# Two mixture-of-experts layers on one core: experts' outputs weighted per slot and added to their tokens' rows in memory, in place of stores, gathers and sums

## The reference, cut to what matters

```python
def hier_moe(h, ...):                       # t: 512 x 1024
    # group by softmax over 4, then the best 2 of the group's 4 experts
    comb = sum(one_hot(expert_id, 16) * weights[..., None])     # 512 x 16, two non-zero a row
    def step(acc, xs):
        wg, wu, wd, cw = xs
        y = (silu(t @ wg) * (t @ wu)) @ wd
        return acc + y * cw[:, None], None
...
h_lat = h_lat + g2 * hier_moe(modulate(h_lat, norm2_g[i], sh2, sc2), ...)   # i = 0, 1
```

## Time and profile before

| | us |
|---|---|
| median of 3 runs | 2244.4 (2242.2 to 2245.37) |
| the profiled execution, its own time | 2244.1 |
| its span, first to last instruction | 2242.5 |
| PE matmuls busy | 2044.5 (91%) |
| DVE busy | 794.9 (35%) |
| ACT busy | 580.6 (26%) |
| POOL busy | 715.6 (32%) |
| mean granted TensorE clock | 0.951 of full |
| transfers: q1 (SP) | 38502 packets, 217.48 MB |
| q0, the only software queue (POOL's) | 27920 packets, 103.82 MB |
| q10 (ACT) | 4608 packets, 16.78 MB |
| data moved | 339.29 MB, 151 GB/s over the span |

### The profile page before, as it was taken

The page is one execution under the profiler, slowest core; times in us unless marked ns, Lnnn a source line. Parts: engine busy times, 40 slices in busy tenths (PEclk is TensorE's granted clock), DMA queues, the critical chain, the costliest instruction groups (busy, mean ns, idle before and its releaser), DMA issues. The chain is left out here.

```text
span 2242.5 us, 23210 instructions
## 1 busy us (share of the span) xinstructions
PE 2044.5 (91%) x7824; PEld 1099.2 (49%) x7824; DVE 794.9 (35%) x1596; ACT 580.6 (26%) x1205; POOL 715.6 (32%) x1055
## 2 busy tenths in 40 slices
PE   7999999999999999999997697995999699778995
PEld 5555555555564555555542355653444344344442
DVE  1434534432123444433315358533222300442223
ACT  3234331234113442221511114521111211111110
POOL 4766766756766676600000031000110100001101
PEclk9999999999999999999998798996999799878997
DMA  7234343234343244360112600016995621055994
GB/s 301 84 113 150 133 145 119 95 127 145 127 150 111 90 166 144 119 266 38 48 75 104 220 16 22 1 46 279 349 366 210 226 75 38 0 226 227 369 366 165
DMA packets 71119, 339.29 MB, mean 151 GB/s; under 512 B 8760, under 2 KB 10230, under 8 KB 56694
## 3 DMA queue, kind: packets, MB, share of 16 engines
q1 hardware_dynamic: 38502, 217.48, 25.7%
q0 software_dynamic: 27920, 103.82, 13.1%
q10 hardware_dynamic: 4608, 16.78, 1.8%
HBM read 292.97 MB, written 45.09 MB: 151 GB/s over the span
## 5 line engine op out<-in xcount | busy, mean ns | idle before, releaser
L386 PE MATMUL psA<-gB,ring 128*128 128x512 f32 x1024 | 455.1, 597 | 0.0
L324 POOL TENSOR_TENSOR wm<-wm,cs 128x256 f32<-128x256 f32 x448 | 266.3, 627 | 135.4 <-DMA wm<-in_mod_w 134.8
L386 PEld LDWEIGHTS psA<-gB,ring 128*128 128x128 f32 x1024 | 189.5, 190 | 223.8 <-issue 223.8
L328 POOL TENSOR_TENSOR wm<-wm 128x256 f32<-128x256 f32 x336 | 243.8, 753 | 31.1 <-issue 23.1
L378 PE MATMUL psA<-ring,gB 128*128 128x384 f32 (+1 forms) x768 | 242.9, 474 | 1.2 <-ACT gB L665 1.2
L378 PEld LDWEIGHTS psA<-ring,gB 128*128 128x128 f32 x768 | 144.6, 190 | 92.0 <-issue 6.8
L1326 POOL DMA_INDIRECT arena<-xs_scratch,idx x4 | 3.9, 965 | 446.7 <-issue 446.7
L842 DVE COPY probT<-psT 128x512 f32<-128x512 f32 x96 | 65.9, 686 | 159.4 <-PE psT L367 159.4
L1460 PE MATMUL psSO<-wreg,arena 128*128 128x512 f32 x256 | 115.3, 593 | 1.9 <-DVE arena L1986 1.9
L1445 PE MATMUL psA<-wreg,arena 128*128 128x512 f32 x256 | 114.9, 602 | 0.0
L1402 PE MATMUL psA<-wreg,mixT 128*128 128x512 f32 x256 | 113.1, 602 | 1.6 <-issue 0.8
(11 more groups left out here) (283 smaller groups left out, 2790.6 us busy)
## 6 DMA issues: line engine op xcount, KB each, us to landing
wm<-in_mod_w POOLq DMA_DIRECT2D x56, 1024.0 KB, 7.9
wreg<-in_w_gu SPq DMA_DIRECT2D x16, 2048.0 KB, 8.6
wreg<-in_w_dn SPq DMA_DIRECT2D x32, 1024.0 KB, 12.3
ring<-in_w_qk SPq DMA_DIRECT2D x24, 1024.0 KB, 4.9
mixT<-in_w_gu SPq DMA_DIRECT2D x8, 2048.0 KB, 8.6
aT<-in_w_gu SPq DMA_DIRECT2D x8, 2048.0 KB, 8.5
ys_scratch<-arena ACTq DMA_DIRECT2D x32, 512.0 KB, 9.9
ring<-in_w_v SPq DMA_DIRECT2D x8, 1536.0 KB, 6.9
```

Of the source, the lines that this page charges most:

```text
L324: nc.gpsimd.tensor_tensor(wm[:, b, k], wm[:, b, k], c_all[:, k].to_broadcast([P, MCH]), ALU.mult)
L328: nc.gpsimd.tensor_tensor(wm[:, b, k], wm[:, b, k], wm[:, b, n + k], ALU.add)
L386: m = nc.tensor.matmul(psA[:, n % 2, :], w(i), src[:, k, :], start=(i == 0), stop=(i == len(ks) - 1))
```

## The change

- DVE's `output` multiplies by the slot's weight as well (a scalar per partition, from `wslot1`). The weights per slot come from eight more small products on PE (`wt_ready`).
- `sum`, a tensor in memory (for layer 1 the output itself), is first filled with `h` by POOL, four plain stores of 512 KB.
- After each output POOL issues an indirect transfer that adds the chunk's rows to their tokens' rows of `sum`, by `home`; unused slots get an index beyond the bound and are dropped. One such transfer is issued only when the one before has landed (`summed`), since two chunks can hold the same token.
- POOL's loop runs for every chunk, so it also gathers for chunks n and n+1, which nothing reads.
- ACT's stores, the gathers from `ys`, DVE's sums, the output stores and the fill of `ys` go. After layer 0 SP loads `h` back from `sum`.

The diff, without the declarations of semaphores and tiles:

```diff
@@ -348,9 +347,6 @@
             with pool.Fori(0, 2 * D // (2 * MCH)) as i:
                 pair(slice(0, 1), i * (2 * MCH), 2 * MODW + i * (2 * MCH), 1, DEPTH * pairs + i)
             pool.wait_ge(const_loaded, 48)
-            ys = d["ys"].rearrange("(c p) n -> p c n", p=P)
-            pool.dma_start(ys, qtab[:].rearrange("p (o h) n -> p o (h n)", o=1).to_broadcast(list(ys.shape))).then_inc(ys_filled, 16)
-            pool.wait_ge(ys_filled, 16)
...
+            n = load_experts(0, N_MOE[0])
...
+            sp.wait_ge(summed[0], 16 * n + 64)
+            for t in range(NT):
+                sp.dma_start(h[:, t, :], d["sum"][0][t * P:(t + 1) * P, :]).then_inc(h_back[t], 16)
             for c in range(1, 4):
...
             load_experts(1, N_MOE[1])
-            for t in range(NT):
-                sp.wait_ge(h_ready, NT + t + 1)
-                sp.dma_start(d["out"][t * P:(t + 1) * P, :], h[:, t, :]).then_inc(stored, 16)
-            sp.wait_ge(stored, 16 * NT)
...
 
+                def move(c, b):
+                    nc.gpsimd.tensor_copy(home1[:, b:b + 1], home[:, ds(c, 1)])
+                    nc.gpsimd.tensor_copy(wslot1[:, b:b + 1], wslots[:, ds(c, 1)]).then_inc(home_moved[l], 1)
+
+                for t in range(NT):
+                    pool.wait_ge(n_xn, N_MOE[l] + t + 1)
+                    pool.dma_start(d["sum"][l][t * P:(t + 1) * P, :], h[:, t, :]).then_inc(summed[l], 16)
                 pool.wait_ge(plan_ready, l + 1)
                 pool.wait_ge(xs_stored, 16 * NT * (l + 1))
                 n = chunks(pool)
                 for b in range(2):
                     pool.indirect_dma_start(xg[:, b, :], None, d["xs"], bass.IndirectOffsetOnAxis(idx[:, b:b + 1], 0))\
                         .then_inc(xg_loaded[l][b], 16)
+                for x in (idx, home, wslots):
+                    nc.gpsimd.memset(x[:, CHUNKS:], 0)
+                pool.wait_ge(home_ready, l + 1)
+                move(0, 0)
                 with pool.Fori(0, (CHUNKS + 1) // 2) as i:
                     for b in range(2):
                         c = 2 * i + b
-                        with pool.If(c + 2 < n):
+                        with pool.If(c < n):
                             pool.wait_ge(xt_ready[l][1], c + 1)
                             pool.sem_inc(waited, 1)
                             gather(c + 2, b)
-                pool.wait_ge(y_stored[l], 16 * n + 16)
+                            pool.wait_ge(summed[l], 16 * c + 64)
+                            pool.sem_inc(waited, 1)
+                            move(c + 1, 1 - b)
+                            pool.wait_ge(xg_loaded[l][b], 16 * i + 32)
+                            pool.wait_ge(yc_copied[l], 2 * c + 4)
+                            pool.wait_ge(home_moved[l], c + 1)
+                            pool.sem_inc(waited, 1)
+                            pool.indirect_dma_start(d["sum"][l], bass.IndirectOffsetOnAxis(home1[:, b:b + 1], 0), ysb[:, b, :], None,
+                                                    bounds_check=S - 1, oob_is_err=False, compute_op=ALU.add)\
+                                .then_inc(summed[l], 16)
+                pool.wait_ge(summed[l], 16 * n + 64)
                 pool.sem_inc(waited, 1)
-                for t in range(NT):
-                    for i in range(TOP):
-                        s = NT * i + t
-                        pool.indirect_dma_start(ygat[:, i, t, :], None, d["ys"],
-                                                bass.IndirectOffsetOnAxis(slots[:, s:s + 1], 0)).then_inc(yg_loaded[t], 16)
...
+                    m = nc.tensor.matmul(psS[:, 0, 0:CHUNKS], slot_hot[:, s, :], past[:, s, 0:CHUNKS],
                                          start=(s == 0), stop=(s == TOP * NT - 1))
                 m.then_inc(idx_ready, 1)
+                pe.wait_ge(wt_ready, 2 * l + 1)
+                for s in range(TOP * NT):
+                    m = nc.tensor.matmul(psS[:, 1, 0:CHUNKS], slot_hot[:, s, :], chunk_hot[:, s, :],
+                                         start=(s == 0), stop=(s == TOP * NT - 1))
+                m.then_inc(wt_ready, 1)
...
-                    act.wait_ge(yc_copied[l], 2 * c + 4)
-                    act.dma_start(d["ys"][ds(c * P, P), :], ysb[:, b, :]).then_inc(y_stored[l], 16)
-
-                act.sem_inc(y_stored[l], 16)
                 act.wait_ge(plan_ready, l + 1)
...
                 dve.drain()
-                nc.vector.tensor_tensor(chunk_hot, chunk_hot, each(tokid, CHUNKS), ALU.mult)
+                nc.vector.tensor_tensor(past[:, :, 0:CHUNKS], chunk_hot, each(tokid, CHUNKS), ALU.mult)
...
+                nc.vector.tensor_tensor(chunk_hot, chunk_hot, each(wts[:].rearrange("p i t -> p (i t)"), CHUNKS),
+                                        ALU.mult).then_inc(wt_ready, 1)
                 dve.wait_ge(idx_ready, l + 1)
-                nc.vector.tensor_copy(idx[:, 0:CHUNKS], psS[:, 0, 0:CHUNKS])
+                nc.vector.tensor_scalar(idx[:, 0:CHUNKS], psS[:, 0, 0:CHUNKS], float(S), float(S - 1), ALU.add, ALU.min)
                 dve.drain()
                 dve.sem_inc(plan_ready, 1)
+                nc.vector.tensor_scalar(home[:, 0:CHUNKS], psS[:, 0, 0:CHUNKS], float(S), None, ALU.add)
+                dve.wait_ge(wt_ready, 2 * l + 2)
+                nc.vector.tensor_copy(wslots[:, 0:CHUNKS], psS[:, 1, 0:CHUNKS]).then_inc(home_ready, 1)
...
 
-                    dve.wait_ge(y_stored[l], 16 * c + 16)
+                    dve.wait_ge(summed[l], 16 * c + 48)
+                    dve.wait_ge(home_moved[l], c + 1)
                     for half in range(2):
                         dve.wait_ge(yc_half[l][half], c + 1)
-                        nc.vector.tensor_tensor(ysb[:, b, half * 512:half * 512 + 512], psO[:, half, :],
-                                                gB[:, 4 * l + 2 + half, :], ALU.mult).then_inc(yc_copied[l], 1)
+                        nc.vector.scalar_tensor_tensor(ysb[:, b, half * 512:half * 512 + 512], psO[:, half, :], wslot1[:, b:b + 1],
+                                                       gB[:, 4 * l + 2 + half, :], ALU.mult, ALU.mult).then_inc(yc_copied[l], 1)
...
-            def combine(l, t):
-                dve.wait_ge(yg_loaded[t], 32 * (l + 1))
-                for i in range(TOP):
-                    m = nc.vector.scalar_tensor_tensor(h[:, t, :], ygat[:, i, t, :], wts[:, i, t:t + 1], h[:, t, :],
-                                                       ALU.mult, ALU.add)
-                    if i == 0:
-                        dve.drain()
-                m.then_inc(h_ready, 1)
+            def returned(t):
+                dve.wait_ge(h_back[t], 16)
+                dve.sem_inc(h_ready, 1)
...
+                returned(t)
...
-            for t in range(NT):
-                combine(1, t)
...
-    d["ys"] = nc.dram_tensor("ys_scratch", (THR * P, D), F32, kind="Internal").ap()
+    d["sum"] = [nc.dram_tensor("sum_scratch", (S, D), F32, kind="Internal").ap(), out]
...
```

More of the change, by code:

```diff
@@ L151, in first_block @@
     x_stored = sem("x_stored")
-    ys_filled = sem("ys_filled")
     MPIECE = MACC // 4
@@ L1071, in second_block @@
     xg, xgT, ysb = part(0, 2, D), part(2048, 2, KD, P), part(4096, 2, D)
-    ygat = part(0, TOP, NT, D)
     sg, hid, hidT = part(8192, 2, D_EXP), part(8704, 2, D_EXP), part(9216, 2, D_EXP)
@@ L1132, in second_block @@
     idx1 = sb("idx1", [P, 2], I32)
-    slots = sb("slots", [P, TOP * NT], I32)
+    home = sb("home", [P, CHUNKS + 3], I32)
+    home1 = sb("home1", [P, 2], I32)
+    wslots = sb("wslots", [P, CHUNKS + 3])
+    wslot1 = sb("wslot1", [P, 2])
     plan = sb("plan", [P, CHUNKS + 4], I32)
@@ L1195, in second_block @@
     yc_copied = per_layer("yc_copied")
-    y_stored = per_layer("y_stored")
-    yg_loaded = [sem(f"yg_loaded{t}") for t in range(NT)]
+    summed = per_layer("summed")
+    home_ready = sem("home_ready")
+    wt_ready = sem("wt_ready")
+    home_moved = per_layer("home_moved")
+    h_back = [sem(f"h_back{t}") for t in range(NT)]
     h_ready = sem("h_ready")
@@ L1203, in second_block @@
     yd_ready = sem("yd_ready")
-    stored = sem("stored")
     T_CTX, T_K, T_Q, T_ATT, T_N2 = 8, 16, 18, 22, (86, 108)
@@ L1267, in load_experts @@
                             load_expert(l, ds(e, 1), b, c + 1)
+                return n
             sp.wait_ge(y2_ready, 8)
@@ L1273, in _ @@
             w_o = d["odd_w_out"].rearrange("(k p) n -> p k n", p=P)
-            load_experts(0, N_MOE[0])
+            n = load_experts(0, N_MOE[0])
             sp.wait_ge(moe_done, 1)
             sp.dma_start(wslot(4096 * ODD_SLOT[0]), w_i[:, :, 0:512]).then_inc(wodd_loaded[ODD_SLOT[0]], 16)
+            sp.wait_ge(summed[0], 16 * n + 64)
             for t in range(NT):
-                sp.wait_ge(yg_loaded[t], 32)
+                sp.dma_start(h[:, t, :], d["sum"][0][t * P:(t + 1) * P, :]).then_inc(h_back[t], 16)
             for c in range(1, 4):
@@ L1425, in experts @@
                 for s in range(TOP * NT):
```

(14 more changed lines are left out.)

## The result

The changed kernel took 2647.9 us (median of 4 runs, 2641.5 to 2652.4) against 2244.9 before: a ratio of 1.179, 95% interval 1.176 to 1.182. It is slower by 18%, where 16% was forecast. The profiled execution took 2645.1 us, with a span of 2643.5.

What follows compares the result with a forecast made beforehand. PE was taken to set the time, with transfers close behind. Span 2242.5 + 374.0 (stalls with clock) + 5.1 + 2.5 - 2.0 - 17.5 = 2604.6; forecast 2606 us, range 2490 to 2770.

Steps and rivals of the forecast that it cites:

- Thirteen stalls a layer, each from scatter to gather: Expert loops: gathers 3 to 15 each wait behind a scatter; 26 gaps, 12.5 us each, 9.7 for chunk 15.
- L: Landing time of the gather inside a stall, put at 8.5 us beside weight loads and 5.7 for chunk 15.
- The clock: After each of 26 gaps PE restarts at half speed for 3.5 to 5 us; 2.1 us lost each.
- The h stores: Start of each expert stage: four stores on POOL's queue delay the xs stores; +5.1 us layer 0, +2.5 layer 1.
- End of layer 0: After PE's last product of layer 0: h ready at the same time, DVE's sums gone; -2 us, within 4 either way.
- End of layer 1: Kernel's end: final gathers, sums and stores go after the last scatter; -17.5 us, between -10 and -19.
- The slow add: Rival, expert loops: a 21 us scatter holds the gather in the shared queue; about 2980 us, chance 15%.
- The clock that does not return: Rival, expert loops: PE runs each whole 11.4 us body at half speed; about 2848 us, chance 6%.
- The gathers that stay hidden: Rival, expert loops: output is copied early enough that scatters do not delay gathers; only edges remain, 2232 us, chance 4%.

Runs made afterwards that it cites:

- the run with POOL's order alone: Changed kernel with gathers 2 and 3 before POOL's loop, then gather c+4 ahead of scatter c, without the two unread gathers; 2236.9 us median of 7 runs.
- the run without rows: Changed kernel with every scatter index beyond the bound, so scatters are issued and complete but carry no rows; 2595.7 us.
- the plain copy: Changed kernel with the scatter writing its rows over instead of adding them; 2627.5 us.
- Keeping the clock: Changed kernel with 15 idle products on PE in the 14 us gaps and 10 in each layer's one short gap; 2599.3 us.
- that with 11 idle products: Changed kernel with 11 idle products on PE after the down products of chunks 0 to 12, inside the stall; 2651.2 us.

## Why the prediction was right, by its own steps

The time, 2647.9, lies in the range (2490 to 2770), 42 us above the forecast of 2606. The mechanism is the one forecast, and the run with POOL's order alone shows it by taking it away: 411 us for the order of one engine's program. Two terms, the gather's landing and the end of layer 1, were sized too small. The terms, with what the trace of the changed kernel (span plus 401.0) gives:

- **Thirteen stalls a layer, each from scatter to gather.** Right in number and place. PE waited 366.1 us for gathers, 350.0 of them in the 26 stalls: 13.5 us each where 12.3 (24 at 12.5, 2 at 9.7) was forecast. The stall without weights took 9.71 us in layer 0 and 9.38 in layer 1, forecast 9.7. That hit is part luck: it was 4.3 + 5.4, not 4.0 + 5.7.
- **What was too small in the others.** The gather was issued 4.3 us into the gap, not 4.0: the scatter's issue is 1.6 us, not a gather's 0.96, and the index copy behind it 0.76, not 0.18. And L was 9.6, not 8.5. Two steps behind L failed. I had the loads all done 12.5 us into the gap, 0.6 sooner than before, and the gather landing with them. The down weights still took 12.3 us and landed 13.0 into the gap, and the gather 0.9 later. And I had let the scatter hold the gather by nothing to 1 us; the run without rows puts it at 2.1 us. The gap is thus the mis-sized term of the sum: 1.2 us too short, 26 times, 31 us. The sentences on the skill's rule had named some 34 us for the add, nearly the same number, but the plain copy shows that this is chance: the add took 0.4 us of the landing and 0.6 of POOL's time, and the time fell by 20 us.
- **The clock.** 54.6 us forecast (26 x 2.1). What the two loops lost beyond PE's waits is 405.7 - 350.0 = 55.7, and PE's busy time in them grew by as much, from 372.2 to 427.8. Keeping the clock gave 48.6 in a run whose stalls were slightly longer. The 2.1 a stall is right, but the rows behind it were misread. The two turns that I took for restarts were the second ones of their stages; the chain of the earlier trace rows has the first turn earlier:

```profile
1547.43 1.13 PE psT L1437 x4
```

So from PE's first turn it took 6.3 us to full clock, and from 2027.38 about 7.6, with 0.8 us idle in between. In the stalls it took 3.5 us after the restart at 1644.97 and 6.0 after that at 2461.64. That the mean came out at 2.1 us lost is partly luck.
- **The h stores.** +5.1 and +2.5 forecast; 1.6 in layer 0, and in layer 1 so little that odd mixer and start together came out 1.8 us shorter. The price per byte fits and the number of bytes was wrong: POOL issues each tile's store as its norm is done, and three of four were issued between 1467.7 and 1495.1 and landed in 2.9 us on a free bus, before any weight load. Only the fourth met the weights (issued at 1511.5, landed 10.7 us later), and the wait for the xs stores grew by 1.1 us.
- **End of layer 0.** -2.0 forecast within 4; +1.9.
- **End of layer 1.** -17.5 forecast, -8.9 found, outside my bounds of 10 to 19. The last scatter was issued 5.2 us after PE's last product, as forecast (5.6), and landed in 6.0 us where 3.7 had been allowed; then came 6.7 us in which no row shows anything, for which the forecast had no term. This step failed as put: "the span ends some 9 us after PE's last product" came out as 17.9.

The sum: stalls and clock +405.7 against 374.0, the end 8.6 us worse, all others together 1.4 us better: 31.7 + 8.6 - 1.4 = 38.9, the whole distance from 2604.6 to 2643.5.

**The rivals.** The slow add: no, 10.9 us and never waited for by PE in the loop. The clock that does not return: no, it came back within 3.5 to 6.0 us of each restart read. After the restart at 1644.97 it is 0.50 up to 1648, 0.88 over 1648 to 1650 and 1.00 from there. The gathers that stay hidden: not in this kernel, but that rival's price was near. It gave 2232 for the edges alone; the kernel with the other order took 2236.9.

## What to carry to other kernels

Before an engine's in-order program is given a new wait, ask what stands behind that wait in the same program, and how far ahead its result was issued until then. A prefetch two steps ahead is only that as long as nothing in its engine's queue waits for the step just finished; the cure is to put the later consumer's prefetch in front of the wait, one more step ahead. And a stall on PE is dearer than its length: here each also cost about 2 us of clock (48.6 over 26 by the run that kept it, 55.7 over 26 by what the loops lost).

## What the runs showed of the hardware

- An indirect transfer that adds costs POOL 1.6 us to issue against 1.0 for one that writes, and an uncontended landing of 6.0 us against 3.2, for about 64 rows of 4 KB. The next copy on POOL took 0.76 us behind the adding one and 0.20 behind the writing one.
- With no rows at all (all out of bounds) it landed in 2.7 us without traffic.
- The rows of a scatter hold up the gather issued behind it: beside weight loads it landed in 9.6 us behind a scatter that adds, 9.2 behind one that writes and 7.4 behind one without rows. Without weight loads it took 5.4, 4.2 and 4.4.
- PE's clock was lost in an idle time of 4.7 us as wholly as in one of 14 (turns of 1.97 us after either), and kept through those of 1.0 to 2.1 us. Between these it varied within one run, that with 11 idle products: turns of 1.97 us after an idle time of 2.88, 1.10 after one of 3.65, 1.5 to 1.8 after some of 4.6 to 4.7. The Trainium skill ("TensorE: Matmul & The Clock Gate", in "Why this matters for your kernels") asks to avoid idle gaps between bursts of matmuls, and the trace agrees. What the loss cost afterwards varied with no rule that I can show. In the changed kernel gate and up took 7.4 to 8.0 us after gaps of 13.6 to 14.7 us and 8.1 to 9.0 after those of 9.4 to 12.8, against 7.03 at full clock. But in the run without rows it alternated between some 7.5 and 8.7 after gaps that were nearly all close to 11.8.
- After the last transfer had landed, the span went on for 6.7 us, for 4.0 us where another engine than POOL had the last wait, and for about 1 us in the kernel before, whose last transfers are plain stores of SP.
